# Two readings of a matmul result: ScalarE copies the gate unit to SBUF, and VectorE's convolution taps read the copy

## What is computed

```python
def dwconv(x, w, b, left):
    K, L = w.shape[0], x.shape[1]
    xp = jnp.pad(x, ((0, 0), (left, K - 1 - left), (0, 0)))
    y = b + w[0] * xp[:, 0:L]
    for k in range(1, K):
        y = y + w[k] * xp[:, k:k + L]
    return y

def conv_ffn(z, w_up, conv_w, conv_b, w_down):
    u = dwconv(z @ w_up, conv_w, conv_b, FFN_CONV // 2)     # D_FF = 2816, FFN_CONV = 3
    g, v = jnp.split(u, 2, axis=-1)
    return (jax.nn.silu(g) * v) @ w_down

xl = xl + mods[5] * conv_ffn(zl, ...)                       # layers 0 and 1, 1024 tokens
xc = xc + cmods[5] * conv_ffn(zc, ...)                      # layer 0 only, 256 tokens
```

## Time and profile before

| | |
|---|---|
| median of three runs | 3474.64 us |
| the profiled execution | 3473.35 us, its span 3471.8 us |
| TensorE matmul busy | 3187.3 us, 92% of the span |
| VectorE busy | 1528.6 us, 44% |
| ScalarE busy | 1006.8 us, 29% |
| GpSimd busy | 304.5 us, 9% |
| mean granted TensorE clock | 0.961 of full |

### The profile page before, as it was taken

How to read it: one execution, slowest core, us unless ns; L and a number is a source line. 1 busy time by engine, 2 the same in 40 slices (tenths; PEclk the granted TensorE clock), 3 DMA queues, 4 the chain that set the end, 5 groups by cost and what they waited for, 6 DMA issues and landing times. The chain is left out here.

```text
span 3471.8 us, 41088 instructions
## 1 busy us (share of the span) xinstructions
PE 3187.3 (92%) x17183; PEld 2555.1 (74%) x17183; DVE 1528.6 (44%) x1801; ACT 1006.8 (29%) x1133; POOL 304.5 (9%) x311
## 2 busy tenths in 40 slices
PE   4799799789899999999996999999988999999996
PEld 3566567467688888888885788888876887887885
DVE  3453445431544444444444433333343445444444
ACT  2344443421311111111112433333442222122122
POOL 1000000051000000000002322222211000000001
PEclk7899899889999999999998999999999999999997
DMA  7111211061221111111201011111031111111111
GB/s 268 54 58 63 71 62 52 24 239 40 81 64 61 61 61 61 61 61 61 61 31 59 24 36 53 37 36 36 24 116 42 49 49 49 49 46 46 43 43 49
DMA packets 197361, 215.21 MB, mean 62 GB/s; under 512 B 15538, under 2 KB 172327, under 8 KB 191045
## 3 DMA queue, kind: packets, MB, share of 16 engines
q1 hardware_dynamic: 187861, 160.12, 14.8%
q0 software_dynamic: 9328, 52.59, 4.5%
HBM read 190.27 MB, written 26.34 MB: 62 GB/s over the span
## 5 line engine op out<-in xcount | busy, mean ns | idle before, releaser
L620 PE MATMUL ps<-zH,wH 128*128 128x512 f32 x2240 | 606.8, 371 | 66.2 <-DVE wL L816 43.4
L620 PE MATMUL ps<-zL,wH 128*128 128x512 f32 x2240 | 601.9, 369 | 0.0
L620 PE MATMUL ps<-zH,wL 128*128 128x512 f32 x2240 | 601.4, 368 | 0.0
L620 PEld LDWEIGHTS ps<-zH,wH 128*128 128x128 f32 x2240 | 388.6, 189 | 157.7 <-DVE wL L816 44.2
L620 PEld LDWEIGHTS ps<-zL,wH 128*128 128x128 f32 x2240 | 388.8, 189 | 73.3
L620 PEld LDWEIGHTS ps<-zH,wL 128*128 128x128 f32 x2240 | 388.7, 188 | 73.4
L1242 DVE SCALAR_TENSOR_TENSOR res<-ps,mod,res 128x1024 f32<-128x1024 f32 (+1 forms) x264 | 260.3, 1014 | 245.0 <-PE ps L620 244.9
L630 DVE SCALAR_TENSOR_TENSOR V<-ps,vec,V 128x1023 f32<-128x1023 f32 (+1 forms) x132 | 134.1, 1016 | 406.1 <-ACT V L1165 403.0
L620 PE MATMUL ps<-hH,wH 128*128 128x512 f32 (+1 forms) x880 | 244.8, 376 | 37.4 <-DVEq L1221 20.3
L1149 ACT ACTIVATE wH<-wraw 128x1024 fp32r<-128x1024 f32 x132 | 136.8, 1050 | 433.7 <-PE ps L620 419.6
L620 PE MATMUL ps<-hL,wH 128*128 128x512 f32 (+1 forms) x880 | 241.7, 372 | 0.0
(11 more groups left out here) (197 smaller groups left out, 3871.7 us busy)
## 6 DMA issues: line engine op xcount, KB each, us to landing
wraw<-in_ffn_w_up_dram SPq DMA_DIRECT2D x88, 512.0 KB, 3.9
modw<-in_mod_w_dram POOLq DMA_DIRECT2D x40, 1024.0 KB, 5.2
wraw<-in_ffn_w_down_dram SPq DMA_DIRECT2D x44, 512.0 KB, 3.4
wraw<-in_na_w_in_dram SPq DMA_DIRECT2D x24, 512.0 KB, 4.7
wraw<-in_rg_w_in_dram SPq DMA_DIRECT2D x20, 512.0 KB, 5.3
modring<-in_mod_w_dram SPq DMA_DIRECT2D x8, 1024.0 KB, 13.8
bias<-scratch_bias SPq DMA_DIRECT2D x32, 224.0 KB, 4.2
scratch_yT<-TR POOLq DMA_DIRECT2D x10, 640.0 KB, 3.2
```

The lines of the kernel that those rows point to most:

```text
L620: last = nc.tensor.matmul(ps[:, slot * SLOT + c:slot * SLOT + c + n], w(k), r(k)[:, c:c + n], start=(k == 0 and i == 0), stop=(k == K - 1 ...
```

## The change

```diff
@@ ffn, GpSimd
-            gp.wait_ge(norm2.stats.sum_done, 1)
+            gp.wait_ge(g_conv, KF - 1)
             squares.clear(gp)
@@ ffn, ScalarE, group
                         act.wait_ge(h_ready, 2 * i + j)
                         col = 2 * i + ((0 if kind == "g" else KF) + j)
+                        if part is BODY and (kind, j) == ("g", 0):
+                            nc.scalar.activation(m.acc[:, 0:ntok], src, ACT.Copy).then_inc(copied, 1)
                         nc.scalar.activation(dst[:, 0:ntok], src, ACT.Identity, scale=fcol(m, l, 1, col), bias=fcol(m, l, 3, col)).then_inc(mid, 1)
+                        if part is BODY and (kind, j) == ("g", 0):
+                            act.wait_ge(mid, 4 * i + 1)
+                            act.nop().then_inc(psum_free[u % 2], 1)
                         after(first, i, u0, k + 3, part)
@@ ffn, VectorE, group
-                        src = ps[:, s * SLOT:s * SLOT + ntok]
+                        early = part is BODY and (kind, j) == ("g", 0)
+                        src = m.acc[:, 0:ntok] if early else ps[:, s * SLOT:s * SLOT + ntok]
                         dst = (m.G if kind == "g" else m.V)[:, 0:ntok]
                         dve.wait_ge(mid, u_mid(first, i, part, kind, j))
                         col = 2 * i + ((0 if kind == "g" else KF) + j)
                         taps(nc, dve, order, dst, src, [(-1, fcol(m, l, 0, col)), (1, fcol(m, l, 2, col))], ntok)
-                        dve.nop().then_inc(psum_free[s], 1)
+                        if not early:
+                            dve.nop().then_inc(psum_free[s], 1)
                         dve.nop().then_inc(g_conv if kind == "g" else v_conv, 1)
```

More of the change, by code:

```diff
@@ L1025, in ffn @@
     mod_in, mod_used, mod_row, mod_T, mod_copied = [sem(tag + n) for n in ("mod_in", "mod_used", "mod_row", "mod_T", "mod_copied")]
+    copied = sem(tag + "copied")
     up = t["ffn_w_up"][l].rearrange("(k p) n -> p k n", p=P)
```

## The result

The changed kernel took 3493.77 us (median of five runs, 3493.19 to 3495.24), the kernel before beside it 3475.65 us. The ratio is 1.0052, 95% interval [1.0038, 1.0067]: 18.1 us slower. The forecast was 3489.0 us, range 3482 to 3496. The profiled execution took 3494.03 us, its span was 3492.4 us.

The account below looks back on a forecast made before the run. TensorE was taken to bound the kernel, busy 92% of the span. Ten groups at 0.62 us plus ten at 0.82 us made 14.4 us slower, 3474.64 to 3489.0 us, range 3482 to 3496 us.

Parts of the forecast that it names:

- part 1: In all twenty body groups d1 no longer waits for slot 0; 20.3 us of TensorE idle time vanish there.
- part 2: ScalarE's copy ahead of the middle tap delays VectorE's taps by 1.14 us in layer 0 and 0.93 in layer 1.
- part 3: VectorE's taps reading SBUF instead of PSUM: no gain taken, from rows of 1281 against 1283 ns.
- The rival on this point: VectorE reads SBUF twice as fast: groups 0.71 and 0.24 us faster, 9.5 us in all, 3465 us; chance 4%.
- part 4: The copy delays VectorE's addition of d0, so d2 waits; d3 starts 0.62 us (layer 0), 0.82 us (layer 1) later.
- The clock falls in the new pauses: Rival: clock halves at layer 1's 2.2 us pause ahead of d2, losing 17 us, 3506 us; chance 5%.
- part 5: Delays of ScalarE's split and silu, VectorE's split, SyncE's weight load and GpSimd's clearing: all taken as costing nothing.

Follow-up runs that it names:

- copy only: The changed kernel without ScalarE's early release of slot 0, the taps reading PSUM again, the copy kept in both layers: 3504.32 us, ratio 1.0075.
- second copy: The changed kernel with a second ScalarE copy to acc behind the first in layer 1: 3503.57 us, ratio 1.0079.
- split twice: The changed kernel with VectorE doing the weight split behind the taps of g0 twice in layer 1: 3526.79 us, ratio 1.0138.

## Why the prediction was right, and where its terms were off

- *TensorE's wait for slot 0 vanishes* (part 1): right, d1 waits for nothing in the twenty groups.
- *The copy's price, 1.14 and 0.93 us* (part 2): right; the distance from the copy's start to the middle tap's is 1143.36 - 1142.22 = 1.14 and 3017.94 - 3017.02 = 0.92. The Trainium skill gives a way to the same number ("ScalarE: Activation LUTs", section "What ACT_TABLE_LOAD costs"): 186 ns + 0.833 ns a column with immediate scale and bias, about 93 ns more for each pointer operand, and 93 ns of overlap. As an estimate from that page 1280 columns take 1252 ns. The row says 1242, and the middle tap with two pointers 1.42 us against 1.44 by the page. The trace agrees.
- *Taps from SBUF are no cheaper* (part 3): right, 1284 ns against 1283. The 65 ns for each tap that the prediction works out from the Trainium skill ("VectorE: DVE Perf Modes", section "The TRN2 errata — SBUF-src ops pay a fixed extra latency per instruction") is not there in these shapes, and the measurement decides. The rival on this point puts its turning point at some 30% of the taps' time; 0.62 of 3.64 us is 17%, and 0.82 of 2.60 us is 32%.
- *d2 waits for the addition of d0* (part 4): right in kind, and shown, since moving the split alone reverses the sign. The size was off: 10 x 0.62 + 10 x 0.82 = 14.4 us were forecast, and d0 to d3 grew by 0.52 and 0.70 us (0.44 in the first group of layer 1), 12 us in all. In the same way d2 waited 1.09 and 1.98 us, 30.7 us together, where 1.3 and 2.1, some 34 us, were forecast. The change also takes out one of two semaphore instructions on VectorE behind the taps, and the split follows in 0.14 us where it was 0.25 us. I costed that line of the diff at nothing. Putting it back restored the 0.25 and, within 0.01 us, the forecast's shifts: 0.61 and 0.81 us.
- *The clock falls in the new pauses* was a rival with 5%, at 17 us or more and in all ten groups of layer 1. It held in part beside the forecast: its price of 1.7 us for a fall was about right (1.6), but only four groups of layer 1 had one, 4 x 1.6 = 6.4 us. 12 + 6.4 = 18.4 us, against 18.1 measured. The forecast's mechanism holds two thirds of the loss, this rival one third. That the total lay in the range is partly luck: two errors have opposite signs, 2 us too much for the chain and 6 us too little for the clock. The step that failed is the one that set forecast and rival against each other, all or nothing; they add up.
- *Nothing for the rest* (part 5): right. GpSimd's clearing now runs in layer 1's last body group, from 3362.98 us on, and the weight split beside it took 1.23 us as elsewhere.

Not settled is some 2 us of the profiled spans' difference of 20.6 us, which lies outside the groups; in the medians it does not show. Open too is why one pause of 1.98 us has a fall behind it and the next of the same length has none.

## What to carry to other kernels

Where a buffer's early release goes through a helper's copy, price the copy on the chain of everything that still waits for it: slot 0 was free about 2 us sooner, but slot 1 hung on VectorE's list behind it and became the bound. Before adding work to free a buffer, look at what is queued between the waiting instruction and the next release, and move that first or with it; here the copy paid once the split stood behind the addition of d2 (8.4 us), and with the taps moved too the kernel gained 24.5 us. A pause of TensorE that grows past what the trace has shown at full clock can cost more than its length.

## What the runs showed of the hardware that I had not expected

The clock can fall behind a pause of some 2 us, and does not always. The pause ahead of an output unit in the body groups, and in how many of ten groups of that layer the granted clock fell to 0.50 in the profile:

| kernel, layer | pause us | falls of ten |
|---|---|---|
| split behind d2, layer 1 | 0.9 | 0 |
| changed, layer 0 | 1.09 | 0 |
| before, layer 1 | 1.27 | 0 |
| copy only, layer 0 | 1.88 | 2 |
| changed, layer 1 | 1.98 | 4 |
| change in layer 1 only | 1.98 | 4 |
| semaphore instruction back, layer 1 | 2.08 (2.46 in one group with a fall) | 4 |
| second copy, layer 1 | 2.15 (and 0.59 one unit earlier) | 3 |
| copy only, layer 1 | 2.19 | 3 |
| split twice, layer 1 | 3.24 | 10 |

Before each of these falls the granted clock had been full for tens of microseconds, and then TensorE paused for 1.9 us or more. Pauses of 1.27 us and less had none. Between 1.9 and 2.2 us the number does not rise with the pause, and equal pauses differ; the length alone does not decide there. A fall behind 1.9 to 2.5 us lasted 3.4 us at half clock, and one behind 3.24 us lasted 6.8 us in nine groups of ten.
